# Second block of a fused two-part model: no low halves on GpSimd, the entry's squares on VectorE, new orders for VectorE and ScalarE

## The reference

```
def hybrid_layer(x, norm_w, w_in, conv_w, conv_b, gate_bias, ret_norm_w, mlstm_norm_w, w_out):
    h = rmsnorm_2(x, norm_w)
    proj = jnp.matmul(h, w_in).astype(jnp.float32)
    (aq, ak, av, ag, bq, bk, bv, bg, cq, ck, cv, co, cg, ci, cf) = jnp.split(proj, cuts, axis=-1)
    ya = moba_attention(aq, ak, av) * silu(ag)                      # 8 heads, softmax with slopes
    yb = head_norm(retention(rotate(bq), rotate(bk), bv)) * silu(bg)  # 4 heads
    qk = silu(causal_dwconv(concat(cq, ck)))                        # 4 taps
    yc = head_norm(mlstm(cq_c, ck_c, cv, ci, cf) * sigmoid(co)) * silu(cg)
    return x + jnp.matmul(concat(ya, yb, yc), w_out)

def second_block(...):
    for layer in range(2): x = hybrid_layer(...)
    return rmsnorm_2(x, final_norm_w)
```

## Time and profile before

| | before |
|---|---|
| median of 3 runs (lowest to highest) | 952.76 us (950.24 to 952.79) |
| the profiled execution: its own time; its span | 951.28 us; 950.0 us |
| TensorE busy | 882.6 us (93%) |
| VectorE busy | 414.0 us (44%) |
| ScalarE busy | 309.5 us (33%) |
| GpSimd busy | 39.3 us (4%), 22 instructions |
| a unit's transfer, from issue to landing, median | 4.8 us |
| second block, from the last expert to the end | about 592 to 950 us |

### The profile page before, as it was taken

The page is one execution under the profiler, slowest core; times in us unless marked ns, Lnnn a source line. Parts: engine busy times, 40 slices in busy tenths (PEclk is TensorE's granted clock), DMA queues, the critical chain, the costliest instruction groups (busy, mean ns, idle before and its releaser), DMA issues.

```text
span 950.0 us, 12843 instructions
## 1 busy us (share of the span) xinstructions
PE 882.6 (93%) x5368; PEld 584.2 (61%) x5368; DVE 414.0 (44%) x785; ACT 309.5 (33%) x559; POOL 39.3 (4%) x22
## 2 busy tenths in 40 slices
PE   5999999999989989899898899989899999889996
PEld 3578874444524444244442333988789899778986
DVE  3187952111101101011110111796886859688782
ACT  4352141111101111011110111756276546626652
POOL 0000000000000000000000000031110003011000
PEclk9999999999999999999999989998999999899998
DMA  9999989999999999999999997632234344223321
GB/s 378 422 427 428 364 354 423 407 429 428 427 423 429 428 427 426 428 427 428 426 429 427 427 423 296 267 133 89 96 128 163 129 175 157 96 103 127 140 90 45
DMA packets 25548, 291.43 MB, mean 307 GB/s; under 512 B 2832, under 2 KB 3344, under 8 KB 4240
## 3 DMA queue, kind: packets, MB, share of 16 engines
q1 hardware_dynamic: 25488, 290.58, 74.3%
HBM read 289.52 MB, written 1.05 MB: 306 GB/s over the span
## 4 chain that ended last, share of the span: by engine, by line
PE 60%; DMA 22%; DVE 12%; ACT 3%; issue 2%; SPq 1%; DVEq 0%; ACTq 0%
PE bank L1449 18%; DMA ring<-in_expert_w 17%; PE bank L1003 15%; PE bank L1035 7%; PE bank L388 3%; DMA more<-in_expert_w 3%; DVE lo L1332 3%; DMA ring<-in_ada_w 2%; PE bank L975 2%; PE bank L935 2%; DVE X L358 2%; PE bank L431 1%; PE bank L404 1%; PE bank L1481 1%; DVE rows L671 1%
## 5 line engine op out<-in xcount | busy, mean ns | idle before, releaser
L1003 PE MATMUL bank<-ring,xg 128*64 128x512 f32 x768 | 240.8, 612 | 16.0 <-DMA ring<-in_expert_w 16.0
L1003 PEld LDWEIGHTS bank<-ring,xg 128*64 128x64 f32 x768 | 75.6, 141 | 137.8 <-issue 110.3
L1449 PE MATMUL bank<-HH,hi 128*128 128x256 f32 x424 | 127.2, 300 | 6.6 <-DVE lo L1332 6.6
L1003 PE MATMUL bank<-more,xg 128*64 128x512 f32 x256 | 120.1, 623 | 8.1 <-DMA more<-in_expert_w 8.1
L1449 PE MATMUL bank<-HL,hi 128*128 128x256 f32 x424 | 121.9, 287 | 0.0
L1449 PE MATMUL bank<-HH,lo 128*128 128x256 f32 x424 | 121.7, 287 | 0.0
L1035 PE MATMUL bank<-ring,X 128*64 128x512 f32 x384 | 113.3, 595 | 0.7 <-ACT X L1075 0.7
L1122 DVE TENSOR_TENSOR X<-X,bank 128x512 f32<-128x512 f32 x16 | 11.0, 687 | 233.5 <-PE bank L1003 233.5
L1449 PEld LDWEIGHTS bank<-HH,hi 128*128 128x128 f32 x424 | 83.1, 196 | 13.2 <-issue 12.4
L1332 DVE TENSOR_TENSOR lo<-raw,hi 128x1024 fp32r<-128x1024 f32 (+1 forms) x78 | 84.6, 1120 | 4.3 <-ACT hi L1326 4.2
L1449 PEld LDWEIGHTS bank<-HL,hi 128*128 128x128 f32 x424 | 83.3, 197 | 1.1 <-issue 1.0
(11 more groups left out here) (350 smaller groups left out, 1467.9 us busy)
## 6 DMA issues: line engine op xcount, KB each, us to landing
ring<-in_expert_w SPq DMA_DIRECT2D x68, 2048.0 KB, 26.9
more<-in_expert_w SPq DMA_DIRECT2D x22, 2048.0 KB, 25.4
raw<-in_units SPq DMA_DIRECT2D x38, 1024.0 KB, 4.8
ring<-in_ada_w SPq DMA_DIRECT2D x10, 2048.0 KB, 21.0
ring<-in_expert_w SPq DMA_DIRECT2D x8, 1024.0 KB, 27.2
ring<-in_w_in SPq DMA_DIRECT2D x3, 2048.0 KB, 34.9
more<-in_ada_w SPq DMA_DIRECT2D x2, 2048.0 KB, 27.5
ring<-in_w_out SPq DMA_DIRECT2D x2, 2048.0 KB, 21.9
```

The lines of the kernel that those rows point to most:

```text
L1003: t = pe.matmul(bank[3 + i][64 * x:64 * x + 64, :], xg[q % 2][:, k, o + 64 * x:o + 64 * x + 64], place(at[x])[:, k, :], start=k == 0, stop ...
L1449: t = pe.matmul(ps[:, T * j:T * j + T], part(st), part(mv), start=first and a == 0, stop=last and a == 2, skip_group_check=True)
```

## The change

Four things change in the second block. The low halves of all pieces go to VectorE, and `POOLED`, `pool_low` and `s_lop` are gone. The squares of the entry are made by VectorE (a product of `xT` with itself), no longer by ScalarE; the load of the square root's table (`root_table`) moves from ahead of the residual to behind it. On TensorE the pair of units 0 and 1 is finished ahead of the gate rows' tile, so units finish in order and `finished(U)` becomes U + 1. And the orders of VectorE and ScalarE are written anew.

```diff
-POOLED = tuple(n for n, (l, u, i) in enumerate(PIECES) if i == 1 and u in (4, 7, 10, 13))
...
                     if ahead(U):
-                        act.wait_ge(s_unit, finished(U - 4))
+                        act.wait_ge(s_unit, U - 3)
...
             def residual_act():
-                root_table()
                 act.wait_ge(s_gw, 1)
...
                     if l:
                         take(both, 4)
                         stats_pair(0, 3)
-                        take(both, 2)
+                        take(both, 4)
...
                         t.then_inc(s_st2, 1)
+                        take(both, 2)
+                    spread_pe(11 if l else 6, 0)
                     pe.wait_ge(s_hl, 8 * l + 8)
                     tile(l, 2, 0)
-                    spread_pe(11 if l else 6, 0)
-                    take(both, 2)
...
-                act.wait_ge(s_sct, 4 * NP)
-                for k in range(0, 8, 2):
-                    act.activation(squares[:, k:k + 2, :], xT[:, k:k + 2, :], ACT.Square).then_inc(s_sqx, 1)
+                root_table()
                 for l in range(2):
                     if l == 0:
-                        high(l, 2)
+                        high(l, 3)
                         scale_root(bank[7][:, 0:4:2], s_st2, 1)
-                        high(l, 3, 0)
...
+                    gate(l, "co")
                     stab_exp(l)
-                    high(l, 8, 0)
-                    gate(l, "co")
-                    high(l, 8)
                     m_exp(l, 0)
...
                 for l in range(2):
-                    pool_low(l, 7)
                     rope(l, 0)
                     rope(l, 1)
-                    pool_low(l, 21)
...
+                dve.wait_ge(s_sct, 4 * NP)
+                for k in range(0, 8, 2):
+                    dve.tensor_tensor(squares[:, k:k + 2, :], xT[:, k:k + 2, :], xT[:, k:k + 2, :], ALU.mult).then_inc(s_sqx, 1)
...
-                    turn = rope(l, 0)
-                    take(turn, 2)
                     m_weigh(l, 2)
                     m_weigh(l, 3)
+                    scaled(l, U_BR + 1, br[:, 2:4, :], s_br)
                     den0 = m_norm(l, 0)
                     take(den0, 3)
-                    scaled(l, U_BR + 1, br[:, 2:4, :], s_br)
-                    turn = rope(l, 1)
-                    take(turn, 2)
                     low(l, 9)
+                    for i in range(2):
+                        turn = rope(l, i)
+                        take(turn, 2)
```

More of the change, by code:

```diff
@@ L1297, in made @@
                     if (m, v) == (l, u) and at <= k < at + c:
-                        pooled = sum(x in POOLED for x in range(n))
-                        return (s_lop, pooled + 1) if n in POOLED else (s_lo, n - pooled + 1)
+                        return s_lo, n + 1
             def pieces_up_to(l, u, i):
@@ L1315, in unit_bank @@
                 return bank[{0: 3, 1: 4, 2: 5, 3: 0, 4: 1}[u] if u < 5 and not l else 3 + u % 3]
-            taken = {"high": 0, "low": 0, "pool": 0}
+            taken = {"high": 0, "low": 0}
             def high(l, u, i=3):
@@ L1899, in second_act @@
                     gate_c(l)
+                    y_high(l, 0)
                     a_turned(l, 6)
@@ L1903, in second_act @@
                     high(l, 19, 0)
-                    y_high(l, 0)
                     gate(l, "ag0")
                     y_high(l, 1)
+                    gate(l, "ag1")
+                    high(l, 18)
+                    y_high(l, 2)
                     high(l, 19)
-                    y_high(l, 2)
-                    gate(l, "ag1")
                     y_high(l, 3)
@@ L2174, in second_dve @@
                     if l == 0:
-                        low(l, 2)
-                        take(one, 1)
-                        low(l, 3, 0)
-                        take(one, 1)
                         low(l, 3)
-                        take(one, 1)
+                        take(one, 3)
                     else:
@@ L2186, in second_dve @@
                     chain = gate_chain(l)
-                    take(chain, 1)
                     conv_in(l, 0)
                     conv_in(l, 1)
-                    take(chain, 1)
+                    low(l, 4, 0)
+                    take(chain, 2)
                     low(l, 4)
                     take(one, 1)
-                    low(l, 5)
+                    low(l, 5, 0)
                     tap = [taps(l, j) for j in range(4)]
                     take(chain, 2)
-                    for j in range(4):
+                    low(l, 5)
+                    for j in range(2):
+                        take(chain, 3)
                         take(tap[j], 1)
-                        take(chain, 2)
+                    low(l, 6, 0)
+                    for j in range(2, 4):
+                        take(chain, 3)
+                        take(tap[j], 1)
                     low(l, 6)
-                    for j in range(4):
-                        take(tap[j], 1)
-                        take(chain, 2)
+                    take(chain, 9)
                     take(one, 1)
@@ L2205, in second_dve @@
                         take(tap[j], 1)
-                        take(chain, 2)
-                    take(chain, 9)
+                    gate_columns(l)
+                    low(l, 7, 0)
+                    for j in range(4):
+                        take(tap[j], 1)
                     scaled(l, U_CO, co, s_gm)
-                    low(l, 7, 0)
-                    gate_columns(l)
                     low(l, 7)
@@ L2214, in second_dve @@
                     scaled(l, U_BR, br[:, 0:2, :], s_br)
-                    low(l, 8, 0)
                     m_weigh(l, 0)
@@ L2273, in second_dve @@
                     low(l, 16)
[L2274 to L2275 removed]
                     a_norm(l, 6)
                     a_norm(l, 7)
+                    scaled(l, U_BG, bg, s_gm)
                     low(l, 17)
+                    norm_gate(l, 0)
+                    if l == 0:
+                        for k in range(4):
+                            x_scale(k)
                     y_low(l, 0)
+                    low(l, 19, 0)
+                    scaled(l, U_AG, ag[:, 0:2, :], s_gm)
                     norm_gate(l, 1)
[L2281 removed]
+                    scaled(l, U_AG + 1, ag[:, 2:4, :], s_gm)
+                    a_gate(l, 0)
                     y_low(l, 1)
[L2283 to L2285 removed]
+                    a_gate(l, 1)
+                    low(l, 18)
                     y_low(l, 2)
[L2287 removed]
+                    low(l, 19)
                     y_low(l, 3)
[L2289 removed]
                     if l == 0:
[L2291 removed]
+                        for k in range(4, 8):
                             x_scale(k)
```

53 lines of the change are left out of this document (17 added, 36 removed).

## The result

The changed kernel took **925.12 us** in the median (923.22 to 926.34; one further execution of 2222 us is left out) beside 952.77 us for the kernel before on the same chip: ratio 0.971, 95% interval 0.968 to 0.974, some 27.7 us less. I had said 930.5 (925 to 941). Measured again in another group it took 924.12 us (921.85 to 925.47, six executions), ratio 0.9714 (0.9688 to 0.9739).

What follows compares the result with a forecast made beforehand. TensorE, busy 93%, was taken as the bound, so only its waits and slow clock could be won. Terms summed to 20.7 us, 21.5 with small products: 929.8 from the profiled 951.28; stated 930.5, range 925 to 941.

Steps and rivals of the forecast that it cites:

- The gate chain: Chain ahead of the stabilisers: shortened from 19.0 to 14 us, saving 7.2 us of waits and 4.5 of slow clock.
- the clock behind the first squares: Layer 0's output: the slow group of 24 products behind the 0.90 us wait returns to full clock, 1.4 us.
- Unit 9: The 2.83 us wait ahead of unit 9 goes in both layers, 5.7 us.
- the small products: The stabilisers' small products, run at the low clock before, gain about 1 us more.
- Output: Waits ahead of unit 17 and the output projection go, 3.3 us; layer 0's first squares' wait and clock, 2.3 us.
- New waits: Retention scores (0.6), norm's mean (0.3) and variance (0.6), VectorE having no pause: 1.5 us a layer lost, 3.0 in all.
- Port of GpSimd: GpSimd's rotation would hold up the norm's reciprocal on VectorE, 1 us taken, between 0 and 1.8.
- Entry: Moving the table load removes most of the 0.95 us wait and VectorE makes the squares: net gain 0.7 us.
- The wait of 0.6 us for the scale: At the entry, three low halves standing ahead of the scale would make TensorE wait 0.6 us for it.
- Waits that grow: Rival, chance 0.22: middle-of-layer waits reach 3 us a layer with a clock drop, losing 7.8 us: 938.3 us.
- ScalarE as the bound of the gate chain: Rival, chance 0.08: ScalarE's Abs and Exp set the chain's end, 11.7 us are not won: 942.5 us.
- Slower: Rival, chance 0.04: VectorE paces TensorE from unit 8 on, 12 us lost, about 965; decided by L2019-to-centring taking 6 us more.

Runs made afterwards that it cites:

- taps_back: The changed kernel with the convolution's tap products (and layer 0's copy of `rstd`) back between the gate chain's steps; 922.25 us, ratio 0.9699.
- unpool_only: The kernel before with only `POOLED` emptied, so GpSimd's low halves go to VectorE and all orders stay; 933.74 us, ratio 0.9817.
- tail_back: The changed kernel with the former orders of VectorE and ScalarE from unit 15 to unit 21; 932.28 us, ratio 0.9805.
- pool_back: The changed kernel with the four low halves a layer back on GpSimd; 927.39 us, ratio 0.9747.
- table_early: The changed kernel with only ScalarE's table load back ahead of the residual, first squares still on VectorE; 923.33 us, ratio 0.9715.
- center_early: The changed kernel with the norm's centring on VectorE ahead of unit 11's low halves; 921.30 us, ratio 0.9698.
- pool_taps_back: The changed kernel with both the taps back between the gate chain's steps and four low halves a layer back on GpSimd; 935.72 us, ratio 0.983.
- pe_order_only: The kernel before with only TensorE's part of the change and `finished(U)` as U + 1; 949.79 us, ratio 0.9983.
- center_table: The changed kernel with the norm's centring ahead of unit 11's low halves and the table load at its former place; 923.26 us, ratio 0.9704.
- rope_first: The changed kernel with unit 9's low halves behind both rotations again; 929.47 us, ratio 0.9785.

## Why the prediction was right, and where it was 6 us off

The mechanisms held; the two sizes that were furthest off erred on one side. The time is at the edge of my range, and measured again (924.12 us) it is 0.9 us beyond it.

- **The gate chain** (7.2 + 4.5 us). Right. I had it at 14 us with 2 to spare; it is 14.3, with 2.0 to spare (2.15 less the 0.15 that TensorE needs behind it). The stages that hold it and the slow clock behind it gave 5.3 us in layer 1, where 3.7 + 1.4 (the clock behind the first squares lies there too) had been counted. My account of what was taken out was partly wrong. I counted eight taps, 3.2 us less 1.4 for gaps, and 0.35 for the copy; it was five, worth 1.5 us, and the copy 0.5. That the sums agree, 2.15 and 1.96, is luck. And they were not needed for it (taps_back); the stretch by GpSimd is what had to go: unpool_only's chain is 4.05 us shorter in layer 0 (19.0 to 14.95) and 2.2 in layer 1 (16.8 to 14.6).
- **Unit 9** (5.7). Right: the stage to `r_scores` is 5.8 us shorter in layer 0, 5.9 in layer 1, of which 2.83 is the wait, 2.4 and 2.2 the clock, and the rest the small products, 1.6 us, which I took at 1 us in all.
- **Output** (3.3 + 2.3, less the new waits). Here is where the sum went wrong, in the sizes of two terms. Counting the first squares' 0.90 and all new waits there, my sum has the stages from `r_scores` to the squares shorter by 1.67 + 0.90 - 1.5 = 1.1 us in layer 0 and by 0.2 in layer 1. They are shorter by 3.4 and 2.3: together 4.4 of the 6 us by which the sum (21.5) fell short of the measured 27.7.
- **New waits** (-3.0). 2.2 us too dear: of the three waits only the one at the norm's variance came, 0.41 us a layer. (The one at the retention's scores is in unpool_only, 0.48 us.) VectorE's stretch from the weighing to the end of the centring takes 21.1 us (654.14 to 675.25), what I had, but by luck: the 1 us for GpSimd's port in it was not due, and in its place stands a pause of 1.09 us in which VectorE waits for TensorE's scores (L2019, 666.12), where I had said that it has no pause. But TensorE's work beside it, which I had at some 20 us, takes 21.4 (from 654.11 to 675.55, where the wait begins).
- **Output's own terms.** The other half of the difference is what waits cost beside their length: tail_back loses 4.05 us in a stage with 2.6 us of listed waits, and 3.00 in one with 1.7: 2.8 us in all that a sum of the bracketed idle times leaves out.
- **Port of GpSimd** (1 us a layer in the new waits). Wrong: the reciprocal took 1.75 us beside GpSimd, as much as the one at 667.64 us with no GpSimd beside it; the stretched rows that I went by were of other operations. L676 in pool_back, which began 0.1 us behind GpSimd's instruction, was held to its end. The rule of the Trainium skill that I had weighed (SBUF — State Buffer, Who interferes with whom) has it that such a reciprocal runs free and that who starts first keeps the ports, and the traces agree. L676 too has only one SBUF input and was held; the rule allows for that only in a two-port mode, which its 0.28 us beside 0.40 for the step with two inputs (L659 of the changed kernel) suggests and no run shows.
- **Entry** (0.7). The wait went, and 1.5 us came back as a slow clock that I had not seen coming; in time the two cancel. The wait of 0.6 us for the scale did not come, either with the slow clock or without it (table_early).
- **The rivals.** Waits that grow: none over 0.41 us. ScalarE as the bound of the gate chain: no. The Exp ends 24.5 us behind the entry's first product (center_early) and not 1.9 but only 0.6 us earlier than in before (25.1), and the chain ends in time. Slower: no stage of the changed kernel is longer than in before. The deciding point that I gave for it, 6 us more from L2019 to the centring, was missed by all of it: 21.1.
- What I did not see is how the parts hang together: GpSimd's halves cost 17 us in the old orders and 3 in the new, the taps 0 or (in the medians) 8. Sized from the prediction's rows, pool_back was expected at 933 or more and unpool_only at 940 or more, and both were wrong.

## What to carry to other kernels

Several edits that shorten one chain draw on one margin: find what each lengthens the chain by, and compare the sum with the distance between the chain's end and the waiting engine. Count the instructions that lie inside the chain in the trace, and not in the loop that issues them: here it was five taps and not eight. Any one edit alone measures as nothing or as everything, depending on which side of the margin the others leave it. To locate gains of 0.5 to 5 us, cut the bottleneck engine's timeline at marks that exist in both kernels; the stages repeat to 0.02 us where whole executions scatter by several us. Work on a side engine is priced by what the main engine's instructions take beside it, not by its own share of the span (here 4%).

## What the runs showed of the hardware

- The granted clock fell at the entry without a wait ahead of it: in the changed kernel's profile TensorE's last listed idle time before is the 0.43 us that ends at 593.89 us, and the clock fell between 606 and 608. Of eight profiles without the 1 us wait at the entry's first product, seven show a slow group (4.38 to 5.01 us for 24 products) and one, pool_taps_back, does not; of six with it, two do (4.22 in pe_order_only, 4.43 in center_table) and four don't. What sets it is open; neither the wait nor the engine of the squares does alone. These are one profile each.
- Behind a wait the clock may fall or not: waits of 0.38 and 0.66 us were followed by groups of 4.21 and 4.41 us, waits of 0.64, 1.05 (layer 1 of pool_back) and 1.88 (layer 0 of rope_first) by 3.06, 3.07 and 3.10. The 2.83 us ahead of unit 9 was followed by 3.10 in before, and in layer 1 of pe_order_only by 4.60. One profile doesn't settle whether a wait costs the 1.4 us too.
- The same subtraction of 128x1024 on GpSimd took 5.86 us in one order and 2.41 in another. In the first, VectorE ran three subtractions of its own almost without a pause from 616.64 to 620.45 us, and GpSimd's ended at 622.72, 2.3 us later: it looks as if it had waited for all of them. In layer 1 it took 3.26 us.
